# Prompt scores as three products of upper and lower parts, with two reorderings at the ends of stages

## The reference

```python
s = (jnp.einsum('bqhd,bkhd->bhqk', qn, k_nope)
     + jnp.einsum('bqhr,bkr->bhqk', qp, k_pe)).astype(jnp.float32) * ATTN_SCALE
s = jnp.where(key_pos[None, :] <= q_pos[:, None], s, jnp.finfo(jnp.float32).min)
p = jax.nn.softmax(s, axis=-1)
return jnp.einsum('bhqk,bkhd->bqhd', p, v)
```

## Time and profile before

| | us |
|---|---|
| three runs | 2912.24, 2912.71, 2912.79 |
| median | 2912.71 |
| the profiled execution | 2923.22 |
| its span | 2921.4 |
| PE busy in the span | 2829.9 (97%) |
| DVE, ACT, POOL busy | 1477.7, 736.8, 1015.3 |

### The profile page before, as it was taken

One profiled execution on the slowest core, in us unless ns is written; L12 is line 12 of the kernel. 1 busy time (PEld: TensorE's weight loads), 2 busy tenths in 40 slices (PEclk: granted clock), 3 DMA queues, 4 the chain that ended last, 5 costly groups with the idle time before them and its releaser, 6 DMA issues.

```text
span 2921.4 us, 45631 instructions
## 1 busy us (share of the span) xinstructions
PE 2829.9 (97%) x18894; PEld 2533.1 (87%) x18894; DVE 1477.7 (51%) x2052; ACT 736.8 (25%) x1154; POOL 1015.3 (35%) x603
## 2 busy tenths in 40 slices
PE   7999999999999999999999889999899999999998
PEld 7999999899999984555766589999799999999997
DVE  3535778766666655555344347865652222222226
ACT  2111211454454544454323222010120000000000
POOL 3443334333333314444211123444333333333331
PEclk9999999999999998999999989999899999999999
DMA  4263223565656544222343334353211111111111
GB/s 142 73 197 119 81 85 121 177 168 150 173 162 171 147 138 120 65 65 69 148 184 129 116 129 140 111 182 106 66 37 44 44 45 49 43 43 50 43 50 60
DMA packets 314769, 309.72 MB, mean 106 GB/s; under 512 B 32101, under 2 KB 273002, under 8 KB 312138
## 3 DMA queue, kind: packets, MB, share of 16 engines
q1 hardware_dynamic: 252392, 196.02, 23.7%
q10 hardware_dynamic: 58650, 73.89, 7.5%
q0 software_dynamic: 3584, 37.75, 3.4%
HBM read 229.41 MB, written 78.20 MB: 105 GB/s over the span
## 4 chain that ended last, share of the span: by engine, by line
PE 81%; DVE 11%; ACT 3%; issue 3%; DMA 1%; POOL 1%; ACTq 0%; SPq 0%; POOLq 0%; DVEq 0%
PE ps L969 41%; PE ps L1150 12%; PE ps L1284 4%; DVE cv L2237 3%; PE ps L1308 2%; PE ps L1298 2%; PE ps L1442 2%; PE ps L1418 2%; PE ps L1398 2%; DVE cv L2231 1%; PE ps L1183 1%; PE ps L1187 1%; PE ps L1176 1%; PE ps L1647 1%; DVE cv L2239 1%
## 5 line engine op out<-in xcount | busy, mean ns | idle before, releaser
L776 POOL TENSOR_TENSOR whi<-raw,cst 128x1024 fp32r<-128x1024 f32 x160 | 311.2, 1945 | 1154.1 <-PE ps L969 945.1
L778 POOL TENSOR_TENSOR wlo<-raw,whi 128x1024 fp32r<-128x1024 f32 x160 | 433.0, 2706 | 12.5
L969 PE MATMUL ps<-ahi,whi 128*128 128x352 f32 x1728 | 375.7, 325 | 2.1 <-POOL wlo L778 1.4
L969 PE MATMUL ps<-alo,whi 128*128 128x352 f32 x1728 | 375.9, 326 | 0.0
L969 PE MATMUL ps<-ahi,wlo 128*128 128x352 f32 x1728 | 372.6, 324 | 0.0
L969 PEld LDWEIGHTS ps<-ahi,whi 128*128 128x128 f32 x1728 | 294.7, 189 | 2.7 <-POOL wlo L778 1.7
L969 PEld LDWEIGHTS ps<-ahi,wlo 128*128 128x128 f32 x1728 | 296.9, 190 | 0.0
L969 PEld LDWEIGHTS ps<-alo,whi 128*128 128x128 f32 x1728 | 295.7, 189 | 0.0
L1150 PE MATMUL ps<-xhi,whi 128*128 128x352 f32 x768 | 255.9, 333 | 0.4 <-ACT xraw L1751 0.4
L1150 PE MATMUL ps<-xhi,wlo 128*128 128x352 f32 x768 | 247.9, 323 | 0.0
L1150 PE MATMUL ps<-xlo,whi 128*128 128x352 f32 x768 | 247.7, 323 | 0.0
(11 more groups left out here) (368 smaller groups left out, 5034.0 us busy)
## 6 DMA issues: line engine op xcount, KB each, us to landing
raw<-in_w_in SPq DMA_DIRECT2D x61, 512.0 KB, 5.0
s_a<-d_acum SPq DMA_DIRECT2D x32, 512.0 KB, 7.3
d_xbc<-so ACTq DMA_DIRECT2D x24, 528.0 KB, 2.7
gt<-d_g SPq DMA_DIRECT2D x24, 528.0 KB, 3.6
raw<-in_w_ffn_gate SPq DMA_DIRECT2D x22, 512.0 KB, 3.8
raw<-in_w_ffn_up SPq DMA_DIRECT2D x22, 512.0 KB, 3.7
raw<-in_w_ffn_down SPq DMA_DIRECT2D x22, 512.0 KB, 3.5
d_z<-zo ACTq DMA_DIRECT2D x16, 528.0 KB, 4.8
```

What stands on the lines that cost most here:

```text
L776: pool.tensor_tensor(whi[s][:, :], raw[:, u], ones[:, 0:1].broadcast_to([P, UNIT]), ALU.mult).then_inc(sem("unit_hi"), k["unit_hi"].adds(1))
L778: pool.tensor_tensor(wlo[s][:, :], raw[:, u], whi[s][:, :].bitcast(F32), ALU.subtract).then_inc(sem("unit_split"), k["unit_split"].adds(1))
L969: last = pe.matmul(ps[0:m, 3 * b + c, 0:width], w(j), x[:, j, at:at + width], start=i == 0, stop=i == n - 1)
```

## The change

It has three parts beside the moves of buffers that make room for them.

1. From the second pair on, a score chunk is three products of rounded parts in place of one fp32 product. ACT makes the upper parts of the next pair's queries and keys (`upper_parts`) behind its later blocks 1, 2, 3 and 5, DVE the lower parts (`lower_parts`) behind its later blocks 2, 3, 4 and 6, each 96x1024, four a pair. The queries and keys are loaded on a semaphore of their own (`qk_full`), for which ACT waits; PE's first score of a pair waits for the four lower parts. The first pair is computed as before (`whole`).
2. The gated products of the first group stand in the last sequence, ahead of DVE's wait for the output; its sums of squares stand behind that sequence and ahead of the copies of the folded output. ACT's fourth square waits until all outputs are ready, since its buffer lies on one that is read until then.
3. The last down product does the first half of tiles 0 to 3 ahead of the wait for the second weight unit.

```diff
-        def scores(pp, G, i, first=False):
+        def scores(pp, G, i, whole=False):
             q, h, b = 4 * G + 3 - i // 2, i % 2, i % 2
-            if G == 0 and i == 0 and not first:
-                pe.wait_ge(sem(f"head_full{pp}"), k[f"head_full{pp}"].next(96))
+            if G == 0 and i == 0 and not whole:
+                pe.wait_ge(sem(f"head_full{pp}"), k[f"head_full{pp}"].next(32))
+                pe.wait_ge(sem("qk_lo"), k["qk_lo"].next(4))
...
-                pe.matmul(ps[:, first_bank + c // 512, 0:w], qb[pp][h][:, q * P:(q + 1) * P], kb[pp][h][:, c:c + w], start=True, stop=True)
+                bank = ps[:, first_bank + c // 512, 0:w]
+                if whole:
+                    pe.matmul(bank, qb[pp][h][:, q * P:(q + 1) * P], kb[pp][h][:, c:c + w], start=True, stop=True)
+                else:
+                    (qh_, kh), (ql, kl) = qkh[pp][h], qkl[pp][h]
+                    for part, (x, y) in enumerate(((qh_, kh), (qh_, kl), (ql, kh))):
+                        pe.matmul(bank, x[:, q * P:(q + 1) * P], y[:, c:c + w], start=part == 0, stop=part == 2)
...
+    SPLITS = (1, 2, 3, 5)
...
+        def upper_parts(pp, i):
+            h, t = divmod(i, 2)
+            if i == 0:
+                act.wait_ge(sem(f"qk_full{pp}"), k[f"qk_full{pp}"].next(64))
+            act.activation(qkh[pp][h][t][:, :], (qb, kb)[t][pp][h][:, :], ACT.Copy).then_inc(sem("qk_hi"), k["qk_hi"].adds(1))
...
                 if i == 1 and not final:
                     head_out(1, pair - 1)
+                if more and i in SPLITS:
+                    upper_parts(1 - pp, SPLITS.index(i))
...
+        def lower_parts(pp, i):
+            h, t = divmod(i, 2)
+            dve.wait_ge(sem("qk_hi"), k["qk_hi"].next())
+            dve.tensor_tensor(qkl[pp][h][t][:, :], (qb, kb)[t][pp][h][:, :], qkh[pp][h][t][:, :].bitcast(F32), ALU.subtract).then_inc(sem("qk_lo"), k["qk_lo"].adds(1))
...
                 if i % 2 == 0:
                     turned(0, 3 - i // 2)
+                if more and i - 1 in SPLITS:
+                    lower_parts(1 - pp, SPLITS.index(i - 1))
...
+                if g == 0 and j == 3:
+                    act.wait_ge(sem("olat_ready"), NB)
...
             for i in (7, 9, 11, 13) if more else ():
                 keys_out(i)
+            if not more and stop >= 7:
+                gated(0, 4)
             dve.wait_ge(sem("olat_ready"), k["olat_ready"].next())
...
+        if stop >= 7:
+            add_pairs()
+            add_all()
         dve.wait_ge(sem("end_turned"), k["end_turned"].next())
...
-        if stop >= 7:
-            gated(0, 4)
-            add_pairs()
-            add_all()
...
+        pe.wait_ge(sem("unit_split"), k["unit_split"].next())
+        last_half(0, 0)
+        pe.wait_ge(sem("res_free0"), k["res_free0"].next())
+        last_half(1, 0)
+        last_half(2, 0)
+        pe.wait_ge(sem("res_free1"), k["res_free1"].next())
+        last_half(3, 0)
+        pe.wait_ge(sem("unit_split"), k["unit_split"].next())
         for i in range(9):
-            last_down(i)
+            if i >= 4:
+                pe.wait_ge(sem("tile_read"), k["tile_read"].next())
+                last_half(i, 0)
+            last_half(i, 1)
+            sum_onto(i)
```

More of the change, by code:

```diff
@@ L402, in build @@
     NBK = NPG // 2
[L403 removed]
+    prb = ar("prb", [P, NBK + 1, P])
+    at_prt = ar.at + 704
+    ar = Arena(at_prt)
+    prt = ar("prt", [P, NBK + 1, P])
     oseq = ar("oseq", [P, NB, KL])
@@ L429, in build @@
     NQ = SEQ // P
+    qkh, qkl = [], []
+    for pp, homes in enumerate(((at_whi, at_ukt), (at_split, ar.at))):
+        ars = [Arena(at) for at in homes]
+        qkh.append([[ars[h](f"{t}h{pp}{h}", [QH, SEQ], F32R) for t in "qk"] for h in range(2)])
+        qkl.append([[ars[h](f"{t}l{pp}{h}", [QH, SEQ], F32R) for t in "qk"] for h in range(2)])
     ar = Arena(low)
@@ L675, in _ @@
                 sp.dma_start(dst, src).then_inc(sem("late_full"), k["late_full"].adds(16))
-        with looped(sp, HEADS // 4 - 1, {k["s_ready"]: 32, k["o_ready"]: 4} | pairs(k, {"head_full": 96})) as i:
+        with looped(sp, HEADS // 4 - 1, {k["s_ready"]: 32, k["o_ready"]: 4} | pairs(k, {"head_full": 32, "qk_full": 64})) as i:
             for pp in range(2):
                 sp.wait_ge(sem("s_ready"), k["s_ready"].next(16))
-                queries_keys(pp, i * 2 + 2 + pp, f"head_full{pp}")
+                queries_keys(pp, i * 2 + 2 + pp, f"qk_full{pp}")
                 sp.wait_ge(sem("o_ready"), k["o_ready"].next(2))
@@ L1315, in later_rows @@
             for i in range(8):
-                scores(pp, 1, i)
+                scores(pp, 1, i, final)
                 if i % 2 == 0:
@@ L1633, in _, with last_half, sum_onto @@
         pe.wait_ge(sem("f_split"), k["f_split"].next(2))
-        def last_down(i):
+        def last_half(i, s):
             n = P if i < 8 else NS
             at, bank = slice(i * P, i * P + n), (6, 0, 2, 4)[i % 4]
[L1639 to L1650, removed]
+            for m in range(6):
+                j, part = divmod(m, 3)
+                w, x = ((whi, fhi), (whi, flo), (wlo, fhi))[part]
+                pe.matmul(ps[0:n, bank + s, :], x[:, j, at], w[s][:, j * 512:(j + 1) * 512], start=m == 0, stop=False)
+        def sum_onto(i):
+            n = P if i < 8 else NS
+            at, bank = slice(i * P, i * P + n), (6, 0, 2, 4)[i % 4]
             for e in range(KT):
@@ L1892, in head_out, with later_rows @@
             act.dma_start(d_att[bass.ds(pair * P, P), G * 512:(G + 1) * 512], att[:, G * 512:(G + 1) * 512]).then_inc(sem("att_stored"), k["att_stored"].adds(16))
-        def later_rows(pair, final=False):
+        def upper_parts(pp, i):
[3 more added lines that the diff above has]
+            act.activation(qkh[pp][h][t][:, :], (qb, kb)[t][pp][h][:, :], ACT.Copy).then_inc(sem("qk_hi"), k["qk_hi"].adds(1))
+        def later_rows(pp, pair, final=False, more=True):
             for i in range(8):
@@ L1926, in _ @@
         act.sem_inc(sem("ssm_over"), 1)
-        later_rows(0, True)
+        k["qk_full1"].n += 32
+        later_rows(0, 0, True)
         with looped(act, HEADS // 4 - 1, {k["m_ready"]: 32, k["t_ready1"]: 24, k["pt_read1"]: 24, k["o_ready"]: 4,
-                                          k["att_stored"]: 64} | pairs(k, {"s_read": 16, "o_read": 2})) as i:
+                                          k["att_stored"]: 64} | pairs(k, {"s_read": 16, "o_read": 2, "qk_full": 64}) | {k["qk_hi"]: 8}) as i:
             earlier_rows(i * 2)
-            later_rows(i * 2 + 1)
+            later_rows(1, i * 2 + 1)
             earlier_rows(i * 2 + 1)
-            later_rows(i * 2 + 2)
+            later_rows(0, i * 2 + 2)
         earlier_rows(HEADS // 2 - 2)
-        later_rows(HEADS // 2 - 1)
+        later_rows(1, HEADS // 2 - 1, more=False)
         earlier_rows(HEADS // 2 - 1, False)
@@ L2509, in keys_out, with gated @@
             dve.tensor_copy(dst, ps[:, 4 + i % 3, :].rearrange("p (r n) -> p r n", n=P)).then_inc(sem("keys_read1"), k["keys_read1"].adds(1))
+        def gated(j0, j1):
+            for j in range(j0, j1):
+                dve.wait_ge(sem(f"yt_full{j % 2}"), k[f"yt_full{j % 2}"].next(32))
+                dve.tensor_tensor(yz[:, j], yt[j % 2][:, :], gt[j % 2][:, :], ALU.mult).then_inc(sem(f"yt_free{j % 2}"), k[f"yt_free{j % 2}"].adds(1))
         def sequence(b, q, more):
@@ L2559, in _ @@
         sequence(1, NB - 1, False)
[L2560 to L2564, removed]
         def add_pairs():
```

28 lines of the change are left out of this document (16 added, 12 removed).

## The result

| | before | after |
|---|---|---|
| median of 18 runs, us | 2912.75 | 2920.36 |
| lowest, highest | 2908.82, 2918.36 | 2914.47, 2929.99 |
| profiled execution, its span | 2923.22, 2921.4 | 2922.57, 2920.8 |

The ratio of after to before is 1.0026, 95% interval 1.0017 to 1.0035: the change made the kernel slower by 7.6 us, where I had forecast 4 us faster. The two profiled executions seem to say "no change". But that of before was itself an odd one, 11 us long in one stage (fifth experiment), so I compare stages with the second profile of before taken there (2910.28 us). Of the executions of experiment 1 one took 4422.71 us at a mean clock of 0.574; it is in no ratio, and without it the median there would be 2899.44.

The account below looks back on a forecast made before the run. TensorE, busy for 97% of the span, was taken as the bound. Attention +9, gated group -10 and last down product -3 gave -4 us on the profiled execution, about 2919, less 10.5 for the median: 2909 us, range 2895 to 2927.

Parts of the forecast that it names:

- Part 1, the products: Prompt's attention scores: three rounded products for one fp32 product save 2.2 us of TensorE's work a pair, seven pairs.
- The rule of the Trainium skill: Score starts: weight loads are pulled ahead, so a pair would lose 16 exposed starts, some 1.6 us; the sum kept them.
- the walk: Prompt's attention: engine queues stepped through with the profile's durations; 37.3 us a pair before, 38.6 after, ending 9 us later.
- Part 2, the ring: Attention's later rows, score banks freed by VectorE and ScalarE: making parts there gives net +1.3 us a pair, 38.6 us.
- the three stands: Each pair's later rows: TensorE stands 1.9, 0.8 and 1.0 us where it stood 0.5.
- the clock falls in the ring: Attention's later rows: standing drops TensorE's clock, some 2 us in each of seven pairs, +14, 2923 us; chance 0.23.
- the 40 us: Attention's pair period: one over 40 us, or under 36.5, makes the prediction wrong.
- Part 3: Gated group moved in front of the last sequence's output: square sums 10.7 us earlier, taken as -10 us.
- My lower bound of -7: Gated group's move: gain of only 7 us if the longer stand drops the clock for the folding.
- The late output: Last sequence: the sum for the output comes 1.6 us later behind the moved gated products, and TensorE behind it.
- Part 4: Last down product: three more first halves cover the weight split, -3 us, bounds -2 to -4.7.
- The offset: Whole run: median 10.5 us below the profiled execution, the same difference applied after, so 2919 gives 2909.

Follow-up runs that it names:

- fifth experiment, experiment 5: The kernel before, unchanged, profiled once more; 2910.28 us (before 2911.41), one run.
- experiment 1: The kernel before with the two reorderings alone (gated group earlier, four first halves of the last down product), without the split scores; 2899.69 us, ratio 0.9952.
- experiment 8: As 3, parts made in the earlier rows, but scores computed in fp32; 2901.73 us, ratio 0.9970.
- 3: After, with parts made half a pair earlier, in the earlier rows of the pair in front (second pair's parts unmoved); 2895.13 us, ratio 0.9941.
- 7: After, with parts made as there in the later rows, but scores computed in fp32; 2912.65 us, ratio 1.0009.
- 12: After, with extra unread fp32 products (512 and 384 columns) ahead of the fifth later score alone; 2909.18 us, ratio 0.9992.
- 9: As 6, with 28 tiny unread fp32 products ahead of TensorE's first load; 2883.02 us, ratio 0.9908.
- 6: As 3, with gated products dealt out: two ahead of the last output's sum, two behind it, additions later; 2890.38 us, ratio 0.9928.

## Why the prediction was wrong, step by step

**Part 1, the products: right.** 128 columns cost 0.11 each, so 0.33 for three, and a score's first load stays exposed (0.34 us from its first product's start to the second's at 1242.36, 0.23 later), as the row had it. The rule of the Trainium skill (TensorE: Matmul & The Clock Gate, section "Step-by-step: what each phase is for") would, as the prediction read it, have had this load pulled ahead; the trace of after disagrees here too. Saved: 1.7 us a pair where the ring is free (experiment 8 against 3), 1.1 with the parts in the later rows (7 against 12); I had 2.2 less what the ring hides, and the walk for those two cases gave 1.6 and 1.1.

**Part 2, the ring: right in kind, 2 us too dear.** With the clock held a pair takes 38.3 us, 1.0 more than before where I had 1.3: the three stands are 1.57, 0.57 and 0.64 us and not 1.9, 0.8 and 1.0. Six such distances are +6.1 us, what lies in front of them +1.6, what lies behind them -0.6: +7.1 in place of +9. That 12's stage is 8.8 us above before, close to my 9, is luck: 2.4 us of it are its filling's and its own fall's.

**The step that failed** is the choice between that and the rival "the clock falls in the ring". I gave it 0.23 and held against it that each stand is shorter than the one of 3.1 us that was seen to drop the clock. That was a sample of one, and an upper bound taken for a threshold, so the sum had nothing for the clock. In after it fell in four of six pairs, at 1.4 to 3.0 us each, 10.2 us in the stage and 9.9 in the runs (12 against after). Three pairs were over the 40 us that I had named as a sign of being wrong. The rival's own size, 14 us, was too high, since not every pair fell.

**Part 3: -6.7 us in place of -10** (fold to squares -7.7, the fold 1.0 us later behind the last sequence's turned weights). My lower bound of -7 named the cause, a longer stand that drops the clock for the folding. The late output was put at 1.6 us, and TensorE stood 1.3 us longer for it. In 1 TensorE was later by itself, so nothing waited for the moved products, and the part brought its 10 (7.2 for 19.7 us, less 2.7 us in front of the fold): by the luck of that execution.

**Part 4: -4.1 for -3.** VectorE starts on its first tile 9.05 us behind the first product, as worked out (9.06); its tiles are 4.16 apart and not 4.25, eight times 0.09. The other 0.4 us are before's: 53.0 us in its second profile, 52.6 in the first, by which I reckoned.

**Not in the sum: the place of the code.** The three products add 146 instructions ahead of the last network's loop; the loop is then fetched anew in each pass, with 3.2 us of stops. By the averages above the place is worth 5.7 of the +7.4 us between the square sums and the last down product; the rest is made of waits that differ from one execution to the next, and I haven't split it.

Added up: 7.1 + 10.2 - 6.7 - 4.1 + 7.4 = 13.9 us; less 0.9 for the earlier first score and 0.8 by which the samples' attention was shorter in front of those turned weights it is 12.2, against 12.3 by the profiles and 7.6 by the medians. The two profiles lie 2.2 us above and 2.5 below their medians.

**The offset.** I took the profiled run's 10.5 us above its median for a constant. It was one execution's own (experiment 5): 12 stops of 4.0 us in all, and slower small products around them (2.2 us for 64 in place of 1.34). All other profiles lie within 6 us of their medians, on both sides.

## What to carry to other kernels

When work moves between engines, ask first in which stretch the busiest engine is bound by its own work, and put it there: the same copies and subtractions cost 2 us a pair in one half of the ring and nothing in the other. A stand that is new on TensorE has two prices, its length and the clock behind it; the second can be as large, and a little useless work inside the stand shows which it is. Before a profile serves as the base of a sum, compare it with the median, and if it lies outside the runs, take another.

## What the runs showed of the hardware

- Behind a stand of 1.57 us among rounded products the granted clock fell to 0.50 for some 3.3 us in four of six pairs of after, and behind one of 1.4 us in three of four. Six stands of 1.30 us among fp32 products (7) never dropped it, those of 0.56 to 0.65 us not in 3, 9 and 12 but once in 6. What decides it is open.
- Adding 1.5 us a pair of products that nobody reads made a kernel about 10 us faster (12 against after).
- 28 products at the start changed how often a loop 2200 us later is fetched: 42 packets behind 2200 us or 5. The kernel's list of instructions has 864 products in that loop, which runs five times. A packet is 2.38 MB / 145 = 16 KB. The Trainium skill (Runtime: NRT & Kernel Launch, section "Instruction fetch mechanics") says that instructions come in blocks of 16 KiB, with which the packets agree, and that TensorE holds 2048 instructions. It also says that only two blocks are held; the 5 packets of experiment 9 for the five passes of that loop speak against it.
- A VectorE subtraction of 1.21 us takes up to 2.8 us beside GpSimd (12), and 1.22 at most once GpSimd's instructions are short.
